# A hybrid stage takes the activations without their norm's factor, and the factor comes in where the sums are read

## The reference

```python
y = xf * lax.rsqrt(jnp.mean(xf * xf, axis=-1, keepdims=True) + NORM_EPS)   # rms_norm
return (y * w.astype(jnp.float32)).astype(x.dtype)
...
proj = h @ w_in          # h = rms_norm(x, mix_norm_w), 512 tokens x 1024
mq, mk, mv, mo, mi, mf, z, xbc, dt_raw, dq, dk, dv = jnp.split(proj, split_idx, axis=-1)
...
xbc = jax.nn.silu(causal_dwconv(xbc, conv_w, conv_b))
```

## Time and profile before

| | before |
|---|---|
| median of 3 runs (lowest, highest) | 3405.39 us (3403.52, 3412.49) |
| profiled execution: its own time | 3405.64 us |
| its span | 3403.4 us |
| mean granted TensorE clock | 0.947 |
| TensorE busy | 3124.8 us, 92% of the span |
| VectorE busy | 1641.5 us, 48% |
| ScalarE busy | 1040.0 us, 31% |

### The profile page before, as it was taken

The page is one execution under the profiler, slowest core; times in us unless marked ns, Lnnn a source line. Parts: engine busy times, 40 slices in busy tenths (PEclk is TensorE's granted clock), DMA queues, the critical chain, the costliest instruction groups (busy, mean ns, idle before and its releaser), DMA issues. The chain is left out here.

```text
span 3403.4 us, 41878 instructions
## 1 busy us (share of the span) xinstructions
PE 3124.8 (92%) x17296; PEld 2377.4 (70%) x17296; DVE 1641.5 (48%) x3102; ACT 1040.0 (31%) x2121; POOL 237.3 (7%) x171
## 2 busy tenths in 40 slices
PE   8999989879999999999999769999898899787887
PEld 6777768757888878888788658888686888332333
DVE  5444474364555554555563555444643674311212
ACT  4222245243323243333344333222332553000002
POOL 0000032121000000000121220000000210000000
PEclk9999989779999999999998779999889899899999
DMA  5443421102223222212211102222212004899997
GB/s 191 179 163 147 150 73 50 38 25 75 99 87 115 84 93 86 70 69 81 87 62 38 38 25 87 93 102 90 78 62 75 2 2 174 328 421 421 421 421 308
DMA packets 66164, 443.36 MB, mean 130 GB/s; under 512 B 7476, under 2 KB 7732, under 8 KB 19640
## 3 DMA queue, kind: packets, MB, share of 16 engines
q1 hardware_dynamic: 61056, 423.65, 32.8%
q10 hardware_dynamic: 3224, 10.49, 0.8%
q0 software_dynamic: 1696, 6.55, 0.5%
HBM read 435.16 MB, written 5.51 MB: 129 GB/s over the span
## 5 line engine op out<-in xcount | busy, mean ns | idle before, releaser
L157 PE MATMUL ps<-b,b 128*128 128x512 f32 (+7 forms) x13982 | 2799.8, 394 | 175.8 <-DVE b L167 58.4
L157 PEld LDWEIGHTS ps<-b,b 128*128 128x128 f32 (+3 forms) x13982 | 2097.1, 184 | 846.2 <-issue 321.3
L167 DVE TENSOR_TENSOR b<-b,b 128x1024 fp32r<-128x1024 f32 (+9 forms) x734 | 598.5, 820 | 274.1 <-ACT b L387 162.4
L387 ACT CAST b<-b 128x1024 fp32r<-128x1024 f32 (+2 forms) x408 | 392.0, 962 | 442.7 <-PE ps L157 437.5
L167 DVE TENSOR_TENSOR b<-ps,b 128x64 f32<-128x64 f32 (+5 forms) x617 | 215.3, 363 | 329.4 <-PE ps L157 274.2
L157 PE MATMUL ps<-b 64*64 64x64 f32 (+10 forms) x2848 | 268.0, 283 | 43.8 <-ACT b L1880 26.2
L167 POOL TENSOR_TENSOR b<-b,b 128x1024 fp32r<-128x1024 f32 (+3 forms) x120 | 202.8, 1706 | 1377.6 <-ACT b L387 947.2
L157 PEld LDWEIGHTS ps<-b 64*64 64x64 f32 (+3 forms) x2848 | 224.4, 164 | 83.5 <-ACT b L1880 31.2
L177 DVE SCALAR_TENSOR_TENSOR b<-ps,b 128x512 f32<-128x512 f32 (+3 forms) x272 | 142.4, 545 | 236.3 <-PE ps L157 211.7
L183 ACT ACTIVATE b<-b 128x512 f32<-128x512 f32 (+8 forms) x294 | 156.1, 538 | 236.1 <-DVE b L177 192.7
L167 DVE TENSOR_TENSOR b<-b,ps 128x512 f32<-128x512 f32 (+1 forms) x106 | 71.8, 678 | 280.0 <-PE ps L157 271.6
(11 more groups left out here) (99 smaller groups left out, 559.6 us busy)
## 6 DMA issues: line engine op xcount, KB each, us to landing
b<-in_eg SPq DMA_DIRECT2D x64, 1024.0 KB, 27.3
b<-in_eu SPq DMA_DIRECT2D x64, 1024.0 KB, 27.2
b<-in_ed SPq DMA_DIRECT2D x64, 1024.0 KB, 27.1
b<-in_wg SPq DMA_DIRECT2D x44, 1024.0 KB, 4.8
b<-in_wu SPq DMA_DIRECT2D x44, 1024.0 KB, 4.9
b<-in_win SPq DMA_DIRECT2D x40, 1024.0 KB, 4.8
b<-in_wd SPq DMA_DIRECT2D x48, 768.0 KB, 4.2
b<-in_wmod SPq DMA_DIRECT2D x24, 1024.0 KB, 5.3
```

The lines of the kernel that those rows point to most:

```text
L157: return e.h.matmul(out, l, r, start=start, stop=stop)
L167: return e.h.tensor_tensor(out, a, b, op)
L387: e.h.copy(hi, src).then_inc(*self.S.tick(("hi", i)))
```

## The change

The half step in front of a hybrid stage now makes that stage's operand as it does for another half step, with the hybrid stage's own weights `nm`. The hybrid stage starts with item 0 and does the norm behind it, without the 8 rounds of `scale_dve` and `scale_act`. VectorE reads the `fm` sums (`xbc`, `qk`, `dqk`, 16 in a stage) and the small gate sums and multiplies them by `rstd`. ScalarE still reads the token-major sums (`V1`, `dv`, `z`, `mo`, 10 in a stage), with the factor as a scale per partition (`rt`, or `rth` with the half that stands in front of a tanh), for which it needs two instructions of 256 columns in place of one of 512. `there(i)` names whose semaphore says that sum i has been read.

```diff
+    def pre_act(self, e, c):
+
+        e.wait_ge(self.before.x_there(c))
+        act(e, self.hp(c)[0], self.k.xT[:, c, :], ACT.Copy, scale=self.k.col(f"nm_{self.l}", c)).then_inc(*self.S.tick(("nhi", c)))
+
+    def pre_dve(self, e, c):
+        e.wait_ge(self.S.at(("nhi", c)))
+        hi, lo = self.hp(c)
+        stt(e, lo, self.k.xT[:, c, :], self.k.col(f"nm_{self.l}", c), hi.bitcast(F32), ALU.mult, ALU.subtract).then_inc(
+            *self.V.tick(("h", c)))
+
+    def there(self, i):
+
+        return (self.V if self.items[i].kind == "fm" else self.S).at(("put", i, 0))
...
         yield from self.first()
-        yield "norm", 0
         diff = 0
         for i in range(self.np):
             yield from self.ahead(i)
             yield "sum", i
+            if i == 0:
+                yield "norm", 0
+            yield "read", i
...
             elif name == "norm":
-                self.scale_act(e, B[7], 512, self.hp)
-            elif name == "sum" and i < self.np:
+                self.norm_act(e, B[7], 512)
+                act(e, self.rt, k.ms[:, 0:4], ACT.Sqrt).then_inc(*S.tick("rt"))
+            elif name == "read":
                 it = self.items[i]
                 if it.kind == "fm":
-                    if it.tag[0] == "xbc":
-                        e.wait_ge(V.at("xzero"))
-                    elif it.tag[0] == "dqk":
-                        e.wait_ge(V.at(("skip", 7)))
-                    e.wait_ge(P.at(("sum", i)))
-                    e.h.copy(self.put(i), B[self.bank(i)][:, :]).then_inc(*S.tick(("put", i, 0)))
...
-                    act(e, self.put(i), src, ACT.Copy, scale=half).then_inc(*S.tick(("put", i, 0)))
+                    for t in range(2):
+                        t1 = act(e, self.put(i)[:, t], src[:, t], ACT.Copy, scale=rt[:, 2 * it.half + t:2 * it.half + t + 1])
+                    t1.then_inc(*S.tick(("put", i, 0)))
...
                 self.norm_dve(e, B[7], 512)
-                self.scale_dve(e, 512, k.xT, self.hp, lambda c: k.col(f"nm_{self.l}", c))
-            elif name == "sum" and i < self.np:
+                e.wait_ge(S.at("rt"))
+                ts(e, self.rth, self.rt, 0.5, ALU.mult).then_inc(*V.tick("rth"))
+            elif name == "read":
                 it = self.items[i]
+                if it.kind == "fm":
+                    e.wait_ge(P.at(("sum", i)), S.at("rstd"))
+                    if it.tag[0] == "xbc":
+                        e.wait_ge(V.at("xzero"))
+                    elif it.tag[0] == "dqk":
+                        e.wait_ge(P.at(("ssd", 7)), V.at(("skip", 7)))
+                    tt(e, self.put(i), B[self.bank(i)][:, :], k.rstd, ALU.mult).then_inc(*V.tick(("put", i, 0)))
                 if it.tag[0] == "xbc":
                     self.conv_dve(e, i, 2 * it.tag[1] + it.half)
...
             elif name == "small":
-                self.small_dve(e, B[6], 512)
+                e.wait_ge(P.at("small"), S.at("rstd"))
+                tt(e, self.small_to[0:16, :], B[6][0:16, :], k.rstd[0:16, :], ALU.mult).then_inc(*V.tick("small"))
...
         if a.name[:3] == "ffn":
-            a.pre_next = b.name[:3] == "ffn"
+            a.pre_next = b.name[:3] in ("ffn", "mix") and b.name != "mixb"
```

More of the change, by code:

```diff
@@ L1526, in __init__ @@
         self.alog, self.mms, self.sms, self.dms = al(32), al(16), al(8), al(16)
+        self.rt, self.rth = al(4), al(4)
         self.dcol = al(64)
@@ L1693, in pe @@
                     for j in self.before_in(i, "fm"):
-                        e.wait_ge(S.at(("put", j, 0)))
+                        e.wait_ge(self.there(j))
                     self.fm_pe(e, i, B[self.bank(i)], 512, self.hp, lambda c: V.at(("h", c)))
@@ L1740, in pe @@
                 else:
-                    e.wait_ge(S.at(("put", 13, 0)), S.at(("Es", 7, 3)), V.at("crow"))
+                    e.wait_ge(self.there(13), S.at(("Es", 7, 3)), V.at("crow"))
                 mm(e, B[7][:, :], k.sel[0:4, h * 128:h * 128 + 128], self.Mrow[0:4, :]).then_inc(*P.tick(("bm", h)))
@@ L1822, in pe @@
                 elif i in (2, 3):
-                    e.wait_ge(V.at(("snorm", 3, 0)), S.at(("put", 17, 0)))
+                    e.wait_ge(V.at(("snorm", 3, 0)), self.there(17))
                 elif i < 2:
-                    e.wait_ge(V.at(("mnorm", 3)), S.at(("put", 25, 0)))
+                    e.wait_ge(V.at(("mnorm", 3)), self.there(25))
                 else:
@@ L1941, in act @@
                         e.wait_ge(P.at(("dsum", n - 2)) if n >= 2 else S.at(("Es", 6 + n, 3)))
-                        e.wait_ge(S.at(("put", i, 0)))
+                        e.wait_ge(self.there(i))
                         act(e, k.two[n % 2], self.dqk[:, n, :], ACT.Square).then_inc(*S.tick(("dsq", n)))
@@ L1947, in act @@
                     src = v4(b, 2, 4) if it.tag[0] == "V1" else v3(b, 2)
-                    half = 0.5 if it.tag[0] in ("z", "mo") else 1.0
+                    rt = self.rth if it.tag[0] in ("z", "mo") else self.rt
+                    e.wait_ge(V.at("rth"))
                     if it.tag[0] == "dv":
@@ L1957, in act @@
                         act(e, mof, mof, ACT.Tanh).then_inc(*S.tick("motanh"))
-            elif name == "sum":
+            elif name == "sum" and i >= self.np:
                 c = i - self.np
```

## The result

The changed kernel took 3430.37 us in the median of 4 runs (3426.24 to 3434.50), the kernel before 3404.45 us (4 runs): a ratio of 1.0071, 95% interval 1.0051 to 1.0091. Timed again, with more runs of the kernel before on the same chip, it was 3426.35 us against 3408.97 us (1.0050, 1.0034 to 1.0066) and 3428.36 us against 3408.48 us (1.0054, 1.0035 to 1.0073). So it is slower by 17 to 26 us. I had forecast 3413 us, with a range from 3398 to 3420.

What follows compares the result with a forecast made beforehand. TensorE, busy 92% of the span, was taken as the bound, with some 20 us at each hybrid stage's front as target. Shifts of 3.1 + 3.2 + 1.0 = +7.3 us on 3405.64 us gave 3413 us, range 3398 to 3420.

Steps and rivals of the forecast that it cites:

- The last products, VectorE's pace and GpSimd: End of half steps 1 and 3: VectorE becomes last, last add +5.7 and +7.3 us, TensorE waits about 9 us.
- GpSimd's two splits: Half step's end: weight splits stall VectorE's lo and add, 2.0 us each, 4.0 us a stage; +1.8 in stage 1.
- the small sums: Behind item 0 and the norm: they start at 447.3 and 1690.1 us, shifts of -1.3 and +0.3 us.
- The `xbc` items: Convolutions up to `sA` 0: VectorE's added reads cost +2.7 us a stage; TensorE's wait at `sA` 0 some 7 us.
- the clock's part: At `sA` 0 in stage 1: TensorE waits long enough to lose its clock, +1.5 us on the score products.
- M: Hybrid stage from the first decay products behind `sA` 0 to the attention's `dfin` products; forecast had only part of 0.5 us.
- F as a whole: Hybrid stage from VectorE's first `xT` update in the last blocks to the decay products behind `sA` 0: +3.1 and +3.2 us.
- The reads of `qk` and `dqk`: State-space and mLSTM part, 8 reads a stage on VectorE: cost nothing, since 0.9 us of cover hides 0.69 us.
- Rival C: State-space and mLSTM part: uncovered `qk` and `dqk` reads make TensorE wait, 11.0 us on top, 3424 us; chance 0.18.
- The sum is made for each stage as the shift of three points: Each hybrid stage: shifts at the end of the norm and item 0, the start of `sA` 0, the stage's end.
- TensorE's clock behind `sA` 0: State-space and mLSTM parts: the forecast put no clock cost there; its clock terms stood at item 0 and `sA` 0.

Runs made afterwards that it cites:

- item 0 free: Changed kernel without TensorE's wait for the last add before item 0: 3410.16 us, 1.0003; with the convolutions' first multiply also on ScalarE: 3395.99 us, 0.9957.
- the one with the wait in front of it filled: Changed kernel with 32 products whose result nobody reads in TensorE's wait in front of item 0: 3419.45 us, 1.0037.
- the two with reads on ScalarE: Changed kernel with sums read by ScalarE again, without the factor: all 16 of xbc, qk, dqk 3419.20 us, 1.0023; only qk and dqk 3427.31 us, 1.0049.
- the moved multiply: Changed kernel with the first multiply of each convolution moved from VectorE to ScalarE, TensorE still waiting for the last add: 3413.61 us, 1.0014.
- the fill at `sA` 0: Changed kernel with 16 products whose result nobody reads in TensorE's wait at `sA` 0 of each hybrid stage: 3419.03 us, 1.0025.

## Why the prediction was wrong

**The last products, VectorE's pace and GpSimd.** Right: updates 3.36 us apart (3.35 foreseen), TensorE's wait 8.37 us in stage 1 and 8.28 in stage 2 ("about 9"), item 0 at 436.28 (437.3), with the clock at 0.50 until 439.8 us, and in stage 2 for the first 5.8 us of item 0 (4.3 foreseen). GpSimd's two splits cost 1.0 + 2.1 us in stage 1, where I had put 4.0. I also took nothing off in stage 2 for the 0.6 us that the 1.26 us add of the earlier trace rows had lost already, and 4.0 less 1.3 and 0.8 is 1.9, not 1.8. The transposes of the small sums came 2.79 us earlier than before in stage 1 (the small sums 1.3 foreseen).

**The `xbc` items.** Right, but for the clock's part. The windows have VectorE busy 51.69 us where it was 48.70, and TensorE's wait at `sA` 0 is 5.18 and 4.00 us, not 7. The reads took 5.5 us, but multiplies and adds of the convolutions went from 39.1 to 35.7 us, since the splits fell elsewhere among them. The clock there cost 2.2 us (4.63 against 2.42), for which I had 1.5. From the transposes of the small sums to the start of M it is 54.1 to 54.2 us in all eight stages of the changed kernel, and 49.3 to 49.4 in the kernel before where the clock did not fall at `sA` 0: 4.9 us, and without the clock's 2.2 the 2.7 that I had put on the reads.

**F as a whole:** +2.4 and +3.3 us against the first profile, +2.5 and +4.8 against the mean of four; foreseen +3.1 and +3.2. The mis-sized part is stage 2: the profile from which I worked had lost 2.3 us there (100.81 us, where three others have 98.40 to 98.62), which I took for the kernel's own.

**The reads of `qk` and `dqk`:** right, nothing. VectorE's idle time in front of the decay product behind item 9 went from 2.45 to 1.56 + 0.20 = 1.76 us (1.8 foreseen), as its timeline shows, and the run with these reads on ScalarE was no faster.

```profile
518.13 0.69 DVE L167 TENSOR_TENSOR b<-ps,b 128x512 f32<-128x512 f32 x1 [1.56 <-PE ps L157]
519.02 0.69 DVE L167 TENSOR_TENSOR b<-ps,b 128x512 f32<-128x512 f32 x1 [0.20 <-PE ps L157]
```

Rival C so came nearest to the time, with 3424 us, for a wrong reason: that is luck.

**The step that failed** is "The sum is made for each stage as the shift of three points", with 0.5 us between the start of `sA` 0 and the stage's end, added to "the profiled execution's own time". Its term for TensorE's clock behind `sA` 0 was nothing, and no reason was given. That took TensorE's clock in the state-space and mLSTM parts as it stood in that execution: at 1.00 from 507 to 566 us and at 0.87 from 563 to 630, M at 133.84 and 133.95. These are the shortest M of their stages in all 20 profiles. Other executions of the same kernel have M at 135 to 146 us, and its median over 26 to 30 executions on a chip is 3408 to 3409 us with a spread of 16 to 23 us, where the three that I had been shown spread over 9. Each execution brings its own M, twice, and from the shortest value it can only go up. Against the mean of the four profiles of the kernel before (3409.9 us, and 2.2 around it) my sum would have given 3419 us. Of the 9 us that still miss, 6.3 are M, which was long in the changed kernel every time. No rival and no bound of the range had this in it: the clock stood in my sum only at item 0 and at `sA` 0.

**What stays open** is why it was long every time. In stage 1, M was short (133.9 to 135.0 us) in all four profiles with item 0 free and in the one with the wait in front of it filled. Of the eight profiles with a prepared operand and that 8 us wait left empty, seven were long (the changed kernel's four, the two with reads on ScalarE, the moved multiply), and the one with the fill at `sA` 0 was short. That points to the wait in front, but the kernel before has no such wait (3.83 us) and was long in two of four, and in stage 2 no such line can be drawn: with item 0 free M was 140.38, 141.76, 146.23 and 135.17 us. A fall at `sA` 0 isn't needed for it, as the changed kernel with the moved multiply shows, which has none there (its eight score products take 2.32 us, M 141.66 and 146.37). No run shows what is.

## What to carry to other kernels

Before a gain of some 0.3% is worked out from a trace, look at several executions of the kernel before and at the granted clock of each long stretch: a part in which the clock hangs in the balance is an unknown of its own, and its price belongs in the range even where the change doesn't touch it. When an operand is prepared in the stage before, take along the waits that were made for the old order: the wait for the last add was harmless while everything needed it, and cost some 16 us when only the norm did. A front that gets faster is worth what the next engine in line lets through: free item 0 and a VectorE relieved by one multiply gave 0.996 to 0.998 of the kernel before together.

## What the runs showed of the hardware

- One execution of the same program on the same chip differs from the next by up to 23 us (3400.06 to 3423.05 us in 30), and the trace shows where: stretches of TensorE at a granted clock of 0.50 come in one execution and not in the other at the same products. The Trainium skill (TensorE: Matmul & The Clock Gate, What's actually happening) says that the chip's watch over TensorE's activity doesn't start with the kernel, so that the place of a clock change differs from run to run. The profiles agree, and show more than a shift by a few products: with the program unchanged and TensorE's idle time in M the same 9.0 us, M differs by up to 12.2 us (133.95 and 146.19).
- The busy share hides the clock: in the window of 67 us TensorE is busy for 65.73 us at a granted clock of 0.75 and for 66.16 us at 0.87, 98 and 99%. A busy share of 98% doesn't say that the clock is full.
- VectorE's multiply with one 128x512 SBUF input and two columns took 0.55 us alone and up to 2.62 beside a split of GpSimd. I had only counted instructions with two such inputs. The kernel before has the form too, at 863 ns in the mean of eight from 448 to 507 us, so it was there to be seen.
